# Routed experts of a four-layer block: 32 token slots per expert instead of 64

## The reference

```python
def hier_moe(h, wg, bg, we, be, w1, w3, w2):
    # top-1 of 4 groups (gate = its softmax prob), then top-2 of the 8 experts inside it
    g_sel = argmax(h @ wg + bg);  top_i = top_k(expert logits of g_sel, 2)
    gates = g_gate * softmax(top_l)
    # for each of the 32 experts e, for the tokens xi routed to it:
    hid = silu(xi @ w1[e]) * (xi @ w3[e])      # w1, w3: 1024 x 512
    y   = hid @ w2[e]                          # w2: 512 x 1024
    out[token] += gates * y
```

## Time and profile before

| | us |
|---|---|
| median of 3 runs | 2070.28 (2063.54 to 2070.98) |
| profiled execution | 2064.35, its span 2062.7 |
| PE busy | 1923.7 (93%) |
| DVE, ACT, GpSimd busy | 660.8, 344.6, 81.0 |
| layer 0's expert stage, first product to last sum | 356.4 to 832.0 |
| layer 1's expert stage, first product to last sum | 1031.7 to 1518.0 |
| mean granted clock of PE | 0.977 |

### The profile page before, as it was taken

The page is one execution under the profiler, slowest core; times in us unless marked ns, Lnnn a source line. Parts: engine busy times, 40 slices in busy tenths (PEclk is TensorE's granted clock), DMA queues, the critical chain, the costliest instruction groups (busy, mean ns, idle before and its releaser), DMA issues.

```text
span 2062.7 us, 27695 instructions
## 1 busy us (share of the span) xinstructions
PE 1923.7 (93%) x11890; PEld 1261.9 (61%) x11890; DVE 660.8 (32%) x1540; ACT 344.6 (17%) x749; POOL 81.0 (4%) x88
## 2 busy tenths in 40 slices
PE   6997879999999999999899999999989999899988
PEld 4756754665555555755566666566568884558753
DVE  2657633222212212671312122212233051411192
ACT  1113113000000000222320000000011222311271
POOL 0000200000000001000000000000100000000000
PEclk9997999999999999999999999999999999999999
DMA  9995506999999999664489999999994434046100
GB/s 353 377 283 204 164 2 246 392 428 427 428 427 429 427 427 408 240 238 149 174 351 423 421 428 428 428 423 427 426 340 150 157 133 153 1 146 228 57 1 31
DMA packets 145936, 586.63 MB, mean 284 GB/s; under 512 B 33084, under 2 KB 44480, under 8 KB 121152
## 3 DMA queue, kind: packets, MB, share of 16 engines
q1 hardware_dynamic: 113504, 558.49, 67.3%
q0 software_dynamic: 8256, 16.63, 2.6%
q10 hardware_dynamic: 24096, 10.38, 2.0%
HBM read 571.41 MB, written 25.23 MB: 289 GB/s over the span
## 4 chain that ended last, share of the span: by engine, by line
PE 66%; DMA 20%; DVE 8%; issue 2%; ACT 2%; PEld 1%; SPq 1%; DVEq 0%; PEldq 0%; ACTq 0%
DMA ring<-in_exp_w_dram 19%; PE bank L2100 14%; PE bank L721 14%; PE bank L710 6%; PE bank L2135 6%; PE bank L852 5%; PE bank L2068 3%; PE bank L2430 3%; PE bank L2420 2%; PE bank L2123 1%; DMA ring<-in_ada_w_dram 1%; PE bank L2076 1%; DVE pair_probs L3206 1%; DVE pair_probs L3191 1%; PE bank L1945 1%
## 5 line engine op out<-in xcount | busy, mean ns | idle before, releaser
L2100 PE MATMUL bank<-ring,hidden_room 128*64 128x256 f32 x4096 | 460.6, 380 | 28.5 <-DMA ring<-in_exp_w_dram 25.3
L2100 PEld LDWEIGHTS bank<-ring,hidden_room 128*64 128x64 f32 x4096 | 316.9, 137 | 185.8 <-DMA ring<-in_exp_w_dram 44.3
L721 PE MATMUL bank<-hT,ring 128*128 128x256 f32 x1344 | 291.9, 379 | 2.8 <-DVEq L164 1.4
L721 PEld LDWEIGHTS bank<-hT,ring 128*128 128x128 f32 x1344 | 255.0, 190 | 38.2 <-issue 3.6
L2135 PE MATMUL bank<-ring,hidden_room 128*64 128x512 f32 x1024 | 233.8, 597 | 6.0 <-issue 2.5
L2326 DVE TENSOR_TENSOR hidden_room<-bank,hidden_room 128x256 f32<-128x256 f32 x64 | 27.2, 425 | 471.5 <-ACT hidden_room L2235 471.5
L2135 PEld LDWEIGHTS bank<-ring,hidden_room 128*64 128x64 f32 x1024 | 76.2, 136 | 122.0 <-issue 122.0
L2235 ACT ACTIVATE hidden_room<-bank 128x256 f32<-128x256 f32 x64 | 24.5, 383 | 743.7 <-PE bank L2100 743.7
L2068 PE MATMUL bank<-xn_kept,member 128*64 128x512 f32 x512 | 121.4, 592 | 0.0
L710 PE MATMUL bank<-ring,hT 128*128 128x512 f32 (+2 forms) x288 | 117.7, 570 | 0.0
L2048 POOL DMA_INDIRECT expert_out<-hidden_room,route_spots x60 | 58.5, 975 | 1164.1 <-DVE hidden_room L2340 1150.5
(11 more groups left out here) (590 smaller groups left out, 1887.8 us busy)
## 6 DMA issues: line engine op xcount, KB each, us to landing
ring<-in_exp_w_dram SPq DMA_DIRECT2D x192, 2048.0 KB, 20.8
ring<-in_ada_w_dram SPq DMA_DIRECT2D x24, 2048.0 KB, 20.7
ring<-in_hawk_w_in_dram SPq DMA_DIRECT2D x15, 2048.0 KB, 8.5
ring<-in_even_w_in_dram SPq DMA_DIRECT2D x7, 2048.0 KB, 17.8
ring<-in_gla_w_in_dram SPq DMA_DIRECT2D x6, 2048.0 KB, 23.2
ring<-in_nsa_w_in_dram SPq DMA_DIRECT2D x5, 2048.0 KB, 7.7
expert_out<-kc POOLq DMA_DIRECT2D x16, 512.0 KB, 12.7
ring<-in_even_w_out_dram SPq DMA_DIRECT2D x2, 2048.0 KB, 7.9
```

The costliest lines, as they stand in the source:

```text
L721: last = nc.tensor.matmul(pair[m // 2][0:rows, (m % 2) * T:(m % 2 + 1) * T], w[:, k, m * P:m * P + rows], src[:, k, :], start=(k == 0), st ...
L2100: last = nc.tensor.matmul(bank[2 + q][halves[half], part * FE // 2:(part + 1) * FE // 2], own[:, q, k % 4, k // 4, :], w[:, k, cols], star ...
```

## The change

CAP becomes 32 and NQ = 128 / CAP = 4 replaces the two halves: every product of an expert uses 32 stationary columns and four column groups.

- **Sort**: each quarter of the 1024 channels goes to its own 32 rows; 256 columns are copied, two transposes instead of four, gain and shift over 256 columns.
- **w1 and w3**: `products` takes all 512 columns at once. The eight k steps go round the four groups, so a bank holds four partial sums.
- **Folds**: ACT copies the w1 bank, DVE the w3 bank (both into an order with f outermost), and `turn_hidden` multiplies each block of 128 columns by the constant `fold` (128 x 32), which adds the four partial sums and turns the rows. Silu and the product with the w3 side come behind it.
- **w2**: four groups of 256 columns; `own_y` has 256 columns; stored pieces are 1 KB, four a row; `expert_out` is cleared by 8 DMAs instead of 16.
- **Ring**: the slot of w1 is freed by `up_ready`, directly behind its own products; those of w3 and w2 as before.
- **Order on PE**: w1 of e, sort of e+1, w3 of e, turn of the w1 side, turn of the tokens, turn of the w3 side, w2. In the last expert the turn of the w1 side and `add_late(0)` stand between w1 and w3.
- **Last sums**: `add_late` takes four row groups of 32 with 256 columns and signals once; DVE does `add_rows(0)`, the scaling of the w2 result, `add_rows(1)`, then eight additions of 256 columns.
- **Memory products** in layer 1: PE waits for both copies of ACT behind them, before for the first alone.
- **Head stage**: three dummy products instead of six.

```diff
-CAP = 64
+CAP = 32
+NQ = P // CAP
...
-                        keep_warm(bank[5], 6)
+                        keep_warm(bank[5], 3)
...
-                frees_from = [(hid_ready, lambda e: hid_ready.start + FT * (e + 1)), (hid_ready, lambda e: hid_ready.start + FT * (e + 1)),
+                frees_from = [(up_ready, lambda e: e + 1), (hid_ready, lambda e: hid_ready.start + FT * (e + 1)),
                               (y_done, lambda e: y_done.start + e + 1)]
...
+                            def products(dst, q, w):
+
+                                for k in range(KD):
+                                    last = nc.tensor.matmul(dst[quarters[k % NQ], :], own[:, q, k % 2, k // 2, :], w[:, k, :], start=(k < NQ), stop=(k >= KD - NQ))
+                                return last
+
+                            def turn_hidden(dst, rows):
+
+                                for f in range(FT):
+                                    last = nc.tensor.matmul(dst[:, f * CAP:(f + 1) * CAP], rows[:, f * P:(f + 1) * P], fold, start=True, stop=True)
+                                return last
...
+                                    weights_in(pe, pair, i, q, 0)
+                                    products(bank[2], q, w1).then_inc(up_ready.sem, 1)
+                                    if closing and q == 1:
+                                        pe.wait_ge(up_copied.sem, e + 1)
+                                        turn_hidden(bank[4], own_up).then_inc(up_turned.sem, 1)
+                                        add_late(0)
+                                        weights_in(pe, pair, i, q, 1)
+                                        products(bank[3], q, w3).then_inc(hid_ready.sem, FT)
+                                    else:
                                         sort_tokens(e + 1, 1 - q)
+                                        weights_in(pe, pair, i, q, 1)
+                                        products(bank[3], q, w3).then_inc(hid_ready.sem, FT)
+                                        pe.wait_ge(up_copied.sem, e + 1)
+                                        turn_hidden(bank[4], own_up).then_inc(up_turned.sem, 1)
+                                        turn_tokens(e + 1)
+                                    pe.wait_ge(side_copied.sem, e + 1)
+                                    turn_hidden(bank[7], own_side).then_inc(side_turned.sem, 1)
+                                    weights_in(pe, pair, i, q, 2)
+                                    pe.wait_ge(hidT_ready.sem, e + 1)
...
                                     for f in range(FT):
-                                        for half in range(2):
-                                            last = nc.tensor.matmul(bank[5 + q][halves[half], :], own_hidT[:, q, f, :],
-                                                                    w2[:, f, half * 512:(half + 1) * 512], start=(f == 0), stop=(f == FT - 1))
+                                        for h in range(NQ):
+                                            last = nc.tensor.matmul(bank[5 + q][quarters[h], 0:QC], own_hidT[:, q, f, :],
+                                                                    w2[:, f, h * QC:(h + 1) * QC], start=(f == 0), stop=(f == FT - 1))
                                     last.then_inc(y_done.sem, 1)
...
-                                    pe.wait_ge(memory_kept.sem, memory_kept.at(2 * bounds.index(a) + 1))
+                                    pe.wait_ge(memory_kept.sem, memory_kept.at(2 * bounds.index(a) + 2))
...
+                            def copy_up(e):
+                                act.wait_ge(up_ready.sem, e + 1)
+                                nc.scalar.copy(own_up.rearrange("p (f s) -> p f s", f=FT), bank[2][:, :].rearrange("p (s f) -> p f s", f=FT)).then_inc(up_copied.sem, 1)
...
+                                    dve.wait_ge(hid_ready.sem, FT * (e + 1))
+                                    nc.vector.tensor_copy(own_side.rearrange("p (f s) -> p f s", f=FT), bank[3][:, :].rearrange("p (s f) -> p f s", f=FT)).then_inc(side_copied.sem, 1)
...
+                                    if not closing or q == 0:
+                                        own_tokens(e + 1, 1 - q)
                                     else:
-                                        own_tokens(e + 1, 1 - q)
+                                        add_rows(0)
...
+                                    if closing and q == 1:
+                                        add_rows(1)
```

More of the change, by code:

```diff
@@ L2060, in _ @@
                         with pe.If(fullest <= CAP):
-                            halves = [slice(0, CAP), slice(CAP, 2 * CAP)]
+                            quarters = [slice(h * CAP, (h + 1) * CAP) for h in range(NQ)]
                             def sort_tokens(e, q):
@@ L2066, in sort_tokens @@
                                 for t in range(TT):
[L2067 to L2069 removed]
+                                    for h in range(NQ):
+                                        last = nc.tensor.matmul(bank[0][quarters[h], 0:QC], member[:, q, t, :],
+                                                                xn[:, t, h * QC:(h + 1) * QC], start=(t == 0), stop=(t == TT - 1))
                                 last.then_inc(sorted_out.sem, 1)
@@ L2083, in add_late @@
                                 for t in range(TT):
-                                    for half in range(2):
-                                        last = nc.tensor.matmul(total[t][half][:, :], lateT[halves[half], q, t * P:(t + 1) * P], own_y[halves[half], q, :],
-                                                                start=(q == 0), stop=(q == 1))
-                                        if q == 1:
-                                            last.then_inc(late_sum.sem, 1)
+                                    for h in range(NQ):
+                                        last = nc.tensor.matmul(total[h][:, t * QC:(t + 1) * QC], lateT[quarters[h], q, t * P:(t + 1) * P],
+                                                                own_y[quarters[h], q, :], start=(q == 0 and t == 0), stop=(q == 1 and t == TT - 1),
+                                                                skip_group_check=True)
+                                if q == 1:
+                                    last.then_inc(late_sum.sem, 1)
                             def two_experts(pair, i, peeled, closing=False):
@@ L2094, in two_experts @@
                                     pe.wait_ge(own_ready.sem, e + 1)
-                                    for part, w in enumerate((w1, w3)):
-                                        weights_in(pe, pair, i, q, part)
-                                        for k in range(KD):
-                                            for half in range(2):
-                                                cols = slice(half * FE // 2, (half + 1) * FE // 2)
-                                                last = nc.tensor.matmul(bank[2 + q][halves[half], part * FE // 2:(part + 1) * FE // 2],
-                                                                        own[:, q, k % 4, k // 4, :], w[:, k, cols],
-                                                                        start=(k == 0), stop=(k == KD - 1))
@@ L2112, in two_experts @@
                                         for late_q in range(2):
                                             for t in range(TT):
-                                                for half in range(2):
+                                                for h in range(NQ):
                                                     cols = slice(late_q * T + t * P, late_q * T + (t + 1) * P)
-                                                    last = nc.tensor.matmul(bank[7][halves[half], cols], late[:, late_q, t, :], ident, start=True, stop=True)
+                                                    last = nc.tensor.matmul(bank[7][quarters[h], cols], late[:, late_q, t, :], ident, start=True, stop=True)
@@ L2117, in two_experts @@
                                         last.then_inc(late_turned.sem, 1)
-                                    pe.wait_ge(own_hid_done.sem, e + 1)
-                                    if closing and q == 1:
-                                        add_late(0)
-                                    for f in range(FT):
-                                        for half in range(2):
-                                            last = nc.tensor.matmul(bank[4][halves[half], f * CAP:(f + 1) * CAP], own_hid[:, f::FT],
-                                                                    ident[:, halves[half]], start=True, stop=True)
@@ L2172, in all_tokens @@
                                                                         start=(k == 0), stop=(k == KD - 1))
+                                            if w is w1 and f == FT - 1:
+                                                last.then_inc(up_ready.sem, 1)
                                         last.then_inc(hid_ready.sem, 1)
```

109 lines of the change are left out of this document (51 added, 58 removed).

## The result

The changed kernel took 2038.82 us (median of 4 runs, 2037.46 to 2040.81) against 2067.85 for the kernel before; the ratio is 0.9862, 95% interval 0.9838 to 0.9885. Measured once more beside the experiments it was 2042.16 us (6 runs), ratio 0.9886, 0.9865 to 0.9907. The forecast was 2047 in a range of 2034 to 2060: a gain of 22.9 us against 29.0 in the first measurement and, by the ratio, 23.6 in the second.

The account below looks back on a forecast made before the run. The weight stream was taken to bound the expert stages, leaving gains at their ends: 11.5 + 12.4 + 1.0 - 2.0 = 22.9 us. The profiled 2064.35 becomes 2041.4; from the median 2070.28, 2047, range 2034 to 2060.

Parts of the forecast that it names:

- The bound: Body of both expert stages: weight loads set the pace, 4.9 us each, 14.7 an expert; halving PE's work gains nothing there.
- the 65% that I gave as a sign: Sign of being right: PE's busy share falls to about 65%, with waits for the DMA ahead of every matrix.
- The front end: Start of each expert stage: products begin 1.8 us sooner, first load 5.2 sooner behind them; stream starts 7.0 us earlier per layer.
- The first load as a part by itself: First weight load of each expert stage goes out 1.95 us behind the first product instead of 7.17: 5.2 us.
- The back end: Last landing to end of sums: W + 8.4 us in layer 0; stage gains, stream included, 11.5 and 12.4 us.
- W: Landing of an expert stage's last weight matrix: 819.1 before and 812.1 after in layer 0, 1497.2 after in layer 1.
- 1 us a layer as an allowance: Back end: taken off per layer for PE's slow clock in w2 product, dummies and late sums (0 to 5 us).
- A w2 product of 3.6 us: Sign of being wrong: the w2 product takes 3.6 us, where 2.1 (1.7 to 3.6) was forecast.
- my 0.065: Time in us per 256-column record in four groups, for the w2 product (2.1 us) and the sort (1.05).
- The new order of the last expert: Back end: DVE does the first tile's rows (2.62 us) during the w2 product, the second's beside the late sums.
- The head: Head stage: three dummy products fewer let the next stage start about 1.0 us earlier (0 to 1.9).
- more than forecast: Rival, 6 in 100: layer 1's stream also loses its dips and the head gains in full, 30 to 34 us, 2038.

Follow-up runs that it names:

- a_w3twice: Changed kernel with every w3 product issued twice, the first pass overwritten by the second: 2039.09 us, ratio 0.9879 to the kernel before.
- a_warm_all: Changed kernel with dummy products ahead of all three matrices in every expert but the first two: 2040.24 us, ratio 0.9867 to the kernel before.
- b_light: Kernel before with every second k step of the w1 and w3 products left out: 2059.65 us, ratio 0.9975.
- a_late: Changed kernel with the slot of w1 freed behind both products again, as before: 2041.33 us, ratio 0.9877 to the kernel before.
- b_early: Kernel before with only the slot of w1 freed early, behind its own products: 2058.12 us, ratio 0.997.
- a_warm: Changed kernel with nine dummy products in the last expert, ahead of w1, w3 and w2: 2032.88 us, ratio 0.9845; repeated 2038.26, ratio 0.9860.
- a_roworder: Changed kernel with DVE doing both token tiles' rows ahead of scaling the last w2 result, as before: 2042.03 us, ratio 0.9878 to the kernel before.
- b_dummies: Kernel before with fewer dummies behind the last late sums, 5 instead of 9 in layer 0, 11 instead of 14 in layer 1: 2062.98 us, ratio 0.9983.
- b_head3: Kernel before with three dummy products at the end of the head stage instead of six: 2065.15 us, ratio 0.9995.
- a_head6: Changed kernel with six dummy products at the end of the head stage again: 2044.31 us, ratio 0.9897 to the kernel before.

## Why the prediction was right

*The bound.* Right, and the step on which all hung. PE's work up by 123 us (a_w3twice), its clock up from 0.85 to 1.00 (a_warm_all), its work down by 230 us in the old kernel (b_light; half of L2100's 460.6 on the page of before): none moved the body. From 420 to 760 the DMA engines move 427 to 428 GB/s in every one of these kernels. PE's busy share did not come down to the 65% that I gave as a sign: it is 83% of the span and 71% of the body (242 of 340 us), since at a clock of 0.85 the same work keeps it busy longer.

*The front end.* Sized well: sort 1.05 (1.05 forecast), entry 1.8 and 1.9 (1.8), first product 1.92. The first load as a part by itself gave less than forecast: 1.5 and 0.8 to 2.8 us in the changed kernel, for 2.95, and 2.8 and 1.7 in the old one, for 3.6 and 0 to 3. In a_late that load goes out 4.57 us behind the first product (358.41 against 353.84), so the lead was 2.6 us to begin with. Over the first 30 us layer 0's stream moves 376 GB/s against a_late's 341, a lead of 2.5 us; at the last product 1.5 are left, and why is open. In b_early the load goes out 3.72 us behind the first product, a lead of 3.45, but later the stream dips once:

```profile
367.80:368.80 1.00, 1.00 (x13) 0.79 (x11) 0.00 (x0) 0.00 (x0) 0.34 (x1) 1.00 0.92 197
...
368.80:369.80 1.00, 1.00 (x12) 0.83 (x10) 0.00 (x0) 0.00 (x0) 0.69 (x1) 1.00 0.74 295
```

Over 30 us it moves 342 GB/s against 303 before, a lead of 2.7 us, which is the 2.8 measured.

*The back end.* The right mechanism, with a term mis-sized. From first product to last sum the forecast had 465.9 and 475.7 us; it was 468.7 and 478.6. Of the 2.8 and 2.9 too many, 1.9 and 1.0 come behind W, as the w2 product ran at half clock for 3.6 and 3.5 us instead of 2.1; I had 1 us a layer as an allowance, in the sum but not in the 8.4. The allowance rested on PE being dense in the last expert, and it was not: in layer 0 it waited 1.88, 1.29 and 2.38 us ahead of the three matrices. A w2 product of 3.6 us was one of my own signs of being wrong. It came true, and cost 1.6 to 2.9 us a layer.

The other 0.9 and 1.9 are W itself. I took the last load to land 4.9 behind the one ahead of it; in layer 0 of the changed kernel it came 6.2 behind (800.37 to 806.56). The view of line 364 in the kernel before, window 792 to 795, in which it issues its last load:

```profile
L364 SPq DMA_DIRECT2D ring<-in_exp_w_dram x1: 327/327/327, 793.8 to 793.8; - x1
...
DMA to landing us min/median/max: 26.5/26.5/26.5
```

It landed at 820.3, 6.1 behind the one ahead and not at the 819.1 of the forecast. The stream's gain in layer 0 is then 463.9 less 458.4 us behind the first product, 5.5 for the 5.2 forecast; so W was placed 1.2 us too early, less the 0.3 that the stream gained beyond the forecast. For layer 1's 1.9 the trace of before gives no landing, and they stay open. The wider spacing goes with the gathers. The queues between the last two landings of the changed kernel, layer 0 and layer 1:

```profile
q1 hardware_dynamic: 1280, 1.66, 74.5%
...
q0 software_dynamic: 180, 0.65, 25.6%
```

```profile
q1 hardware_dynamic: 603, 1.65, 67.6%
...
q0 software_dynamic: 239, 0.84, 33.5%
```

The weight queue, 99.3% of 16 engines in the body, has 74.5% and 67.6% here, and GpSimd's queue, with the gathers, the rest.

The rule of the Trainium skill, page "TensorE: Matmul & The Clock Gate", section "HAM oscillation", that bursts which each wait for a DMA start slow, agrees with the trace here in part. The w2 product behind 2.38 us of waiting ran at 0.50, and with dummies in that time (a_warm) at full clock; but the w3 product ahead of it, behind 1.29 us of waiting, took its full-clock 1.92. The price was 1.6 to 2.9 us a layer and not 5, because only the w2 product and, in layer 0, the first dummies behind it (2.77 us) ran slow: the late sums took 1.15 at full clock. That the w2 product takes 1.93 at full clock, 0.060 a record, bears out my 0.065.

*The new order of the last expert.* I put its gain in the wrong place. DVE's new order gives 1 us at most (a_roworder). In the kernel before, the w2 product started 2.1 us behind its landing (822.44 against 820.3), at the end of a chain of 8.3 us that begins on w3's landing. In the changed kernel what begins on w3's landing (800.37) is product, copy, turn and the product with the other side, done at 804.58: 4.2 us. The next landing comes at 6.2, and the w2 product starts on W. That is worth 2.1 us in layer 0. Two parts of the change shorten the chain: silu's turn and the late sums stand ahead of w3's landing, and the w3 product takes 1.92 us in place of 3.67. The shorter product alone would leave some 6.5 us, close to the 6.2, and in layer 1 of b_light, where it had that length, the w2 product did start on its DMA. So how much of the 2.1 us the new order gives is not shown; it was not tried by itself.

*The head.* 1.0 forecast; 0.9 measured, with an interval of -1.4 to 3.5, so this term is not shown.

*Missed.* The 3.1 and 1.0 us behind the sums. In the kernel before PE reached the turns 2.65 and 2.05 us after its last dummy. In layer 0 the trace names nothing that it waited for; in layer 1 it names ACT, whose rows had been ready for 1.00 us (1522.51 + 1.15 = 1523.66, turns at 1524.66). b_dummies moved the start by 2.1 and 1.0 us with nothing but fewer dummies. The dummies of the kernel before, layer 0:

```profile
830.28 4.15 PE L424 MATMUL bank<-kc 128*128 128x256 f32 x18
```

They end at 834.43, 2.45 us behind the sums (831.98). In the changed kernel they end at 813.91 + 4.15 = 818.06, only 1.2 behind the sums (816.85), mostly because the late sums ahead of them take 1.15 us on PE in place of 1.99. So the turns start 3.34 us behind the sums in place of 5.11, on their rows from ACT. These 1.8 us are the change's: the second profile has 3.34 too, and b_head3 and b_early, with the old late sums, 4.83 and 5.11. The other 1.4 of the table's 3.1 are the turns at full clock, 1.97 us in place of 3.37, and they are luck of the profile: b_early has 1.97 as well, and a_head6, on the changed kernel, 3.33. I had read the earlier trace rows as a matter of the clock alone and not asked why PE stood idle ahead of it.

So the total came out near partly because errors cancel. With the 1 us a layer allowed for the clock the forecast had 21.9 us for the expert stages, 3.6 more than the 18.3 they gave in the first profile and 5.7 more than the 16.2 of the second, and it left out the 2.7 behind them that are the change's. The rival "more than forecast" is not borne out. Of the 29.0 us in the first measurement the steps account for 20 to 22 (16.2 to 18.3, 2.7 and the head's 0.9), a little under what the second measurement gave (23.6); the rest is the spread of the runs as far as these profiles tell.

## What to carry to other kernels

Before a faster engine is given credit in a stream-bound stage, ask which first transfer it lets out sooner and what stands between the last landing and the end; the body is worth nothing, as doubling a product or halving it shows in one run. A last landing is better read from its load's issue and time to landing than placed by the usual spacing, since other transfers may share the engines just there. Dummies that hold a clock have two costs to check: whether they are done before the next engine's result is, and what PE still has to get through behind them.

## What the runs showed of the hardware

Behind the last dummy PE stood 1.84 to 2.85 us before it began the turns, in eight cases of five kernels in which the trace names no wait. The dummies stand at the end of a conditional branch there; that leaving it is what takes the time was not tried by itself. In the three longest of these gaps (2.65, 2.65 and 2.85 us) the DMA view has one packet of an instruction queue, q8, and in the other five none; whether PE waited for it is open. Thirty-two products of 256 columns with 32 stationary columns follow each other at 0.060 us at a granted clock of 1.00. A stream that had stood still moved 98, 180 and 344 GB/s in the first three microseconds behind the issue of its first load, and 426 in the fourth (changed kernel, layer 0). The gathered rows, which landed 12.3 us (median) after their issue in the kernel before, took 16.4 in layer 0 of the changed one. The start-up of the program spreads by 7 to 8 us between executions of nearly equal kernels (layer 0's out stage at 311.1 to 318.5 on the old kernel and 308.3 to 316.3 on the new), more than most of what was studied here.
